# mLSTM denominators as four rows of one PSUM bank with one reciprocal in the next stage, and score products issued two steps ahead

## The chip, the cores and the metric

The kernel runs on one core of one Trainium2 chip. The metric is the device time of one execution in microseconds (us). The kernel before takes 2518.95 us, the median of three runs (2518.74 to 2519.68).

A core has a matrix engine (TensorE, "PE" in the profile, with its weight loads as "PEld"), a vector engine (VectorE, "DVE"), a scalar engine (ScalarE, "ACT"), GpSimd ("POOL") and SyncE ("SP"), which here only issues DMAs. Each runs its own instructions in order; semaphores tie them together. PE writes to PSUM, which has eight banks of 128 partitions by 512 floats; everything else lies in SBUF.

## What is computed

The reference is two blocks of a hybrid network, for a sequence of 512 tokens of width 1024. The first block has two layers, and each layer has three mixers: an mLSTM (four heads of width 256), a gated linear attention and a sparse attention. The change touches only the mLSTM and what stands around it. This is its step, which the reference runs chunk by chunk:

```python
bcum = jnp.cumsum(lfj, axis=-1)
dmat = jnp.where(causal, bcum[..., :, None] - bcum[..., None, :] + lij[..., None, :], -jnp.inf)
inter = bcum + m[..., None]
m_row = jnp.maximum(inter, jnp.max(dmat, axis=-1))
w_intra = jnp.exp(dmat - m_row[..., None])
w_inter = jnp.exp(inter - m_row)
s_qk = jnp.einsum('bhld,bhsd->bhls', qj, kj) * w_intra
num = jnp.einsum('bhls,bhse->bhle', s_qk, vj) + w_inter[..., None] * jnp.einsum('bhld,bhde->bhle', qj, C)
den = jnp.sum(s_qk, axis=-1) + w_inter * jnp.einsum('bhld,bhd->bhl', qj, n)
hj = num / jnp.maximum(jnp.abs(den), jnp.exp(-m_row))[..., None]
```

The output of a head is a weighted sum of values (`num`), divided per token by the larger of the absolute sum of weights (`den`) and `exp(-m_row)`. A normalisation over the head's 256 features and two gates follow.

## The kernel before, in words

The kernel computes the mLSTM for all 512 tokens at once, without chunks. Features lie on partitions and tokens along the free dimension. For a head `h` and a block `j` of 128 key tokens it makes a tile of weights `w` of 128 keys by the 512 - 128j queries at or after them. These sixteen pairs (h, j) are the *steps* of `mlstm_stage` (L909). The stage is run twice, once in each layer.

In a step:

- PE makes the scores, k transposed times q, in two matmuls over the head's two halves of 128 features (L939). `scores(n)` writes bank 1 or 2, in turn.
- DVE takes the row `G` of the head, which PE has spread over all partitions (L947, bank 0 or 7), subtracts a number per key and clamps (L999, `arguments`). ACT takes the exponential (L982).
- DVE multiplies scores and exponentials (L1025), masks the first 128 columns (L1028), and signals `w_ready`.
- PE multiplies `w` by the two halves of the values, into banks 3 and 4 (L963, L964: the numerators), and by a matrix of ones, into bank 5 (L967). So bank 5 holds the sum of weights of each token, the same in all 128 partitions.

PE issues `scores(n + 1)` just before it waits for `w` of step n. At j = 1 it also spreads the rows of the next head (`head_rows`): `G` (L947) and `em`, which is exp(-m_row) (L950, bank 6). L950 waits for `em_copied`, since bank 6 still holds the row of the current head until DVE has copied it to SBUF (L1032).

When the first step of the next head has its weights, DVE calls `finish` for the head before: it takes the larger of minus the sum and `em` (L1006), then the larger of the sum and that (L1009), then the reciprocal (L891), and multiplies the two tiles of the head's numerators by it (L895). Only behind that stands L1032. The numerators were copied out of banks 3 and 4 by ACT (L973) into `m.yT`; PE waits for this copy (`num_copied`) before it writes the next head's numerators. For the last head, the reciprocal and the two products are left to the next stage (`mlstm_last`, L898).

The next stage is a `product_stage`: PE multiplies the layer's input by weight granules in three split passes (L276), ACT and POOL split the weights in two parts (L293, L340), and *sides* put other work between. A side is a generator for each engine. PE calls all sides twice per granule (24 matmuls): at its start and at its half. DVE and ACT call theirs once per granule. Within one engine the order is fixed when the program is written: the rest of a side's turn stands behind whatever it waits for. On DVE the sides of this stage start with `mlstm_last`, then `topk_side` (L1366 and L1370, sixteen rounds that find the largest index scores of the sparse attention; L1376 ends it), then `dsa_norms` (L1277), which waits for ACT (L537). PE's L511 belongs to `dsa_norms`. PE uses banks 0 to 3 there; the sparse attention's side uses banks 4 to 6, from turn 12 on. Between two stages all engines meet at a barrier.

The matmuls of the mLSTM are in plain 32-bit floats. The trace shows each as two MATMUL records.

Of the kernel before, what the change touches and what calls it, by code (L numbers as in the profile page):

```python
# [8 lines left out]
ALU = mybir.AluOpType  # L9
# [3 lines left out]
P = 128  # L13
S = 512
# [874 lines left out]
def mlstm_over(m, dve, own, h):  # L889

    own.op(dve.reciprocal(m.rs[:, 2, :], m.rs[:, 1, :]))  # L891
    own.wait()
    for e in range(2):
        y = m.yT[:, 2 * h + e, :]
        own.op(dve.tensor_tensor(y, y, m.rs[:, 2, :], ALU.mult))  # L895


def mlstm_last(m):  # L898

    def vector(dve, sem):  # L900
        own = Chain(dve, sem["last_head"])
        mlstm_over(m, dve, own, ML_H - 1)
        own.wait()
        yield

    return Side(["last_head"], lambda pe, sem: iter(()), lambda act, sem: iter(()), vector)


def mlstm_stage(nc, m, ahead):  # L909
# [3 lines left out]
    em = ab  # L913

    with stage(nc, "rows_ready", "qk_ready", "arg_ready", "exp_ready", "w_ready", "num_done", "pv_done", "num_copied", "den_read",
               "raw_loaded", "high_ready", "low_ready",
               "em_copied", "dve_own") as (block, sem):
# [15 lines left out]
        def _(pe):  # L933
            def scores(n):
                h, j = steps[n]
                if n >= 2:
                    pe.wait_ge(sem["w_ready"], n - 1)
                for kk in range(2):
                    last = pe.matmul(m.ps[:, 1 + n % 2, 0:S - j * P], k[:, 2 * h + kk, j * P:(j + 1) * P],  # L939
                                     q[:, 2 * h + kk, j * P:S], start=(kk == 0), stop=(kk == 1))  # L940
                last.then_inc(sem["qk_ready"], 1)

            def head_rows(h):
# [44 lines left out]
        def _(dve):  # L988
# [13 lines left out]
            def finish(h):  # L1002

                dve.wait_ge(sem["em_copied"], h + 1)
# [1873 lines left out]
```

## Time and profile before

| | |
|---|---|
| median of three runs | 2518.95 us (2518.74 to 2519.68) |
| the profiled execution | 2534.25 us |
| its span, first to last instruction | 2532.5 us |
| PE busy in the span | 2369.5 us (94%) |
| DVE busy | 1214.2 us (48%) |
| ACT busy | 949.6 us (37%) |
| POOL busy | 817.3 us (32%) |
| mean clock granted to PE | 0.966 of full speed |
| first mLSTM stage, from PE's first matmul | 228.16 us |
| product stage behind it, from PE's first matmul | 301.88 us |
| second mLSTM stage, from PE's first matmul | 912.10 us |
| product stage behind it, from PE's first matmul | 984.43 us |

All times within the kernel are of the one profiled execution, counted from its first instruction. The profiled execution is 15.3 us (0.6%) longer than the median of the plain runs, and 1.75 us of it lie outside the span. A row of a timeline gives the start, the length, the engine, the line, the operation with what it writes and reads, and in brackets the engine's idle time before it and who ended it. Matmuls are pipelined, so their lengths overlap: the distance between two starts tells the pace.

### The profile page before, as it was taken

The numbers are of one execution on the slowest core, as the hardware profiler recorded it, in microseconds if no ns is written. First come the engines' busy times: TensorE is split into PE (matmuls) and PEld (weight loads), VectorE is DVE, ScalarE is ACT, GpSimd is POOL, SyncE is SP. The second block draws the span as 40 slices with busy tenths as digits, with TensorE's granted clock in tenths as the row PEclk, the third lists the DMA queues.
The fourth block names the chain that finished last, engine by engine and source line by source line (L and its number), as shares of the span: only waits on it lengthen the run. The fifth ranks groups of instructions, "written<-read, shape, count | busy, mean of one in ns | idle before, by whom it ended". The sixth has DMA issues, their size and how long they took to land. (4 is left out here: it accounts for less than half of the span.)

```text
span 2532.5 us, 39488 instructions
## 1 busy us (share of the span) xinstructions
PE 2369.5 (94%) x16764; PEld 1874.0 (74%) x16764; DVE 1214.2 (48%) x1966; ACT 949.6 (37%) x1385; POOL 817.3 (32%) x364
## 2 busy tenths in 40 slices
PE   5999899999999998999989989998999899999997
PEld 3877587786778866877768758887676678888886
DVE  2254764433332558543431457765454466605524
ACT  3432145544244322454342343332336624212233
POOL 1342033332433411333234322222332344444442
PEclk8999899999999999999999988999899999999998
DMA  3221022221222201222223210000221123323222
GB/s 126 76 92 50 25 83 75 67 76 58 93 77 75 92 34 43 83 76 67 67 67 105 92 34 3 4 3 9 88 72 62 59 89 102 100 93 99 98 94 75
DMA packets 50139, 176.31 MB, mean 70 GB/s; under 512 B 5604, under 2 KB 6188, under 8 KB 49964
## 3 DMA queue, kind: packets, MB, share of 16 engines
q1 hardware_dynamic: 49404, 172.78, 20.6%
q8 instruction: 133, 2.18, 0.4%
q10 hardware_dynamic: 560, 1.00, 0.1%
q14 instruction: 42, 0.34, 0.0%
HBM read 171.65 MB, written 2.11 MB: 69 GB/s over the span
## 5 line engine op out<-in xcount | busy, mean ns | idle before, releaser
L340 POOL TENSOR_TENSOR w_low<-work,w_high 128x1024 fp32r<-128x1024 f32 x310 | 752.9, 2429 | 1433.9 <-ACT w_high L293 1433.9
L276 PE MATMUL ps<-x_high_tiles,w_high 128*128 128x512 f32 x1640 | 665.8, 406 | 29.6 <-DVE x_low_tiles L657 10.5
L276 PE MATMUL ps<-x_low_tiles,w_high 128*128 128x512 f32 x1640 | 647.1, 395 | 0.8 <-DVE x_low_tiles L372 0.8
L276 PE MATMUL ps<-x_high_tiles,w_low 128*128 128x512 f32 x1640 | 647.7, 395 | 0.0
L293 ACT ACTIVATE w_high<-work 128x1024 fp32r<-128x1024 f32 x310 | 327.7, 1057 | 719.3 <-PE ps L276 717.7
L276 PEld LDWEIGHTS ps<-x_high_tiles,w_high 128*128 128x128 f32 x1640 | 312.6, 191 | 129.5 <-issue 54.5
L276 PEld LDWEIGHTS ps<-x_low_tiles,w_high 128*128 128x128 f32 x1640 | 312.7, 191 | 70.5 <-DVE x_low_tiles L383 1.7
L276 PEld LDWEIGHTS ps<-x_high_tiles,w_low 128*128 128x128 f32 x1640 | 312.6, 191 | 67.5 <-issue 5.3
L276 PE MATMUL ps<-arena_parts,w_high 128*128 128x512 f32 x1088 | 347.8, 395 | 13.6 <-POOL w_low L340 5.4
L276 PEld LDWEIGHTS ps<-arena_parts,w_high 128*128 128x128 f32 x1088 | 206.6, 190 | 60.9 <-issue 8.4
L276 PE MATMUL ps<-arena_parts,w_low 128*128 128x512 f32 x544 | 213.9, 393 | 0.0
L276 PE MATMUL ps<-w_high,x_high_tiles 128*128 128x256 f32 x576 | 169.0, 293 | 0.0
L276 PE MATMUL ps<-w_low,x_high_tiles 128*128 128x256 f32 x576 | 163.1, 283 | 0.0
L276 PE MATMUL ps<-w_high,x_low_tiles 128*128 128x256 f32 x576 | 163.0, 283 | 0.0
L444 DVE TENSOR_TENSOR xT_sb<-ps,xT_sb 128x512 f32<-128x512 f32 x40 | 27.6, 692 | 261.5 <-PE ps L276 261.5
L1674 PE MATMUL ps<-work 64*64 64x64 f32 x3584 | 118.8, 225 | 8.1 <-DVE work L1989 7.3
L1674 PEld LDWEIGHTS ps<-work 64*64 64x64 f32 x3584 | 113.9, 140 | 14.9 <-issue 14.8
L276 PEld LDWEIGHTS ps<-w_high,x_high_tiles 128*128 128x128 f32 x576 | 110.3, 192 | 14.0 <-issue 13.6
L276 PEld LDWEIGHTS ps<-arena_parts,w_low 128*128 128x128 f32 x544 | 103.4, 190 | 21.9 <-issue 0.7
L1892 POOL TENSOR_TENSOR work<-work,arena 128x512 f32<-128x512 f32 x40 | 54.6, 1380 | 193.9 <-ACT work L1866 101.2
L276 PEld LDWEIGHTS ps<-w_low,x_high_tiles 128*128 128x128 f32 x576 | 110.4, 192 | 2.5 <-issue 2.2
L276 PEld LDWEIGHTS ps<-w_high,x_low_tiles 128*128 128x128 f32 x576 | 110.4, 192 | 0.0
(428 smaller groups left out, 2855.5 us busy)
## 6 DMA issues: line engine op xcount, KB each, us to landing
work<-w_first SPq DMA_DIRECT2D x180, 512.0 KB, 3.7
work<-w_second SPq DMA_DIRECT2D x134, 512.0 KB, 3.7
xT_sb<-xT SPq DMA_DIRECT2D x8, 256.0 KB, 6.8
outT<-arena SPq DMA_DIRECT2D x8, 256.0 KB, 2.1
arena<-distance_bias SPq DMA_DIRECT2D x4, 256.0 KB, 3.6
small<-small SPq DMA_DIRECT2D x1, 819.5 KB, 4.3
arena<-consts SPq DMA_DIRECT2D x1, 544.0 KB, 3.7
base<-consts ACTq DMA_DIRECT2D x1, 512.0 KB, 5.9
```

Source lines behind the costliest of these rows:

```text
L276: ins = pe.matmul(out, lhsT, rhs, start=(n == 0 and k == 0 and q == 0), stop=(n == unit["granules"] - 1 and k == len(ops[i]) - 1 and q == 2))
L293: act.activation(m.wh[:, split_of(g), :], m.raw[:, raw_of(g), :], ACT.Copy).then_inc(sem["high_ready"], 1)
L340: pool.tensor_tensor(m.wl[:, split_of(g), :], m.raw[:, raw_of(g), :], m.wh[:, split_of(g), :].bitcast(F32), ALU.subtract).then_inc(sem["lo ...
L444: return dict(dve=lambda e, ps, own: e.tensor_tensor(dst, ps, dst, ALU.add))
L1674: ins = pe.matmul(out[HALF[p], cols], lhsT[HALF[p], cols], rhs[HALF[p], cols], start=True, stop=True)
L1892: pool.tensor_tensor(ch(w.L), ch(w.AT), every(w.lev[:, n * 64:n * 64 + 64]), ALU.mult).then_inc(sem[f"lev_ready{w.d}"], 1)
```

## The change

It does four things.

1. The denominators. The matmul with the matrix of ones is replaced by one with a block of four columns (`m.one_column[:, 3 - h:7 - h]`), in which column h is one and the others are zero. So head h adds its sums of weights to row h of bank 5 and zeros to the other rows; the bank collects all sixteen steps of the stage in four rows.
2. `em` is no longer spread over the partitions. L950 and L1032 and the waits around them go, and `finish` goes with its four operations a head. Bank 6 is free.
3. In the next product stage `mlstm_last` makes the larger values and one reciprocal for the four heads, on tiles of 4 by 512. PE spreads the four rows with four matmuls (banks 4 and 6, in turn), and DVE multiplies the eight tiles of numerators by them, from PSUM. DVE does heads 0 and 1 in its second turn and heads 2 and 3 in its third; PE spreads rows 0 and 1 at its fourth call and rows 2 and 3 at its sixth.
4. The scores get a third bank (1, 2 and 6), and PE issues `scores(n + 2)`, no longer `scores(n + 1)`, before it waits for `w` of step n.

Also the first square of `dsa_norms` on ACT no longer waits for `mlstm_last`.

```diff
-def mlstm_last(m):
+def mlstm_last(m, banks):
+    den, em, inv = m.ps[0:ML_H, 5, :], m.rows[0:ML_H, 1, :], m.rs[0:ML_H, 2, :]
 
     def vector(dve, sem):
-        own = Chain(dve, sem["last_head"])
-        mlstm_over(m, dve, own, ML_H - 1)
+        own = Chain(dve, sem["last_own"])
+        own.op(dve.scalar_tensor_tensor(out=inv, in0=den, scalar=-1.0, in1=em, op0=ALU.mult, op1=ALU.max))
         own.wait()
+        own.op(dve.tensor_tensor(inv, den, inv, ALU.max))
+        own.wait()
+        dve.reciprocal(inv, inv).then_inc(sem["den_inv"], 1)
+        for h in range(ML_H):
+            if h % 2 == 0:
+                yield
+            dve.wait_ge(sem["inv_spread"], h + 1)
+            for e in range(2):
+                y = m.yT[:, 2 * h + e, :]
+                dve.tensor_tensor(y, y, m.ps[:, banks[h % 2], :], ALU.mult).then_inc(sem["y_divided"], 1)
+        dve.wait_ge(sem["y_divided"], 2 * ML_H)
         yield
+
+    def tensor(pe, sem):
+        yield from turns(3)
+        pe.wait_ge(sem["den_inv"], 1)
+        for h in range(ML_H):
+            if h >= 2:
+                pe.wait_ge(sem["y_divided"], 2 * (h - 1))
+            pe.matmul(m.ps[:, banks[h % 2], :], m.pick[0:ML_H, h * P:(h + 1) * P], inv, start=True, stop=True).then_inc(sem["inv_spread"], 1)
+            if h == 1:
+                yield from turns(2)
...
@@ mlstm_stage, PE
             def scores(n):
                 h, j = steps[n]
-                if n >= 2:
-                    pe.wait_ge(sem["w_ready"], n - 1)
+                if n >= 3:
+                    pe.wait_ge(sem["w_ready"], n - 2)
...
-                pe.matmul(m.ps[:, (0, 7)[h % 2], :], m.pick[0:ML_H, h * P:(h + 1) * P], G, start=True, stop=True)
-                if h:
-                    pe.wait_ge(sem["em_copied"], h)
-                pe.matmul(m.ps[:, 6, :], m.pick[0:ML_H, h * P:(h + 1) * P], em, start=True, stop=True).then_inc(sem["rows_ready"], 1)
+                pe.matmul(m.ps[:, (0, 7)[h % 2], :], m.pick[0:ML_H, h * P:(h + 1) * P], G, start=True, stop=True).then_inc(sem["rows_ready"], 1)
 
             head_rows(0)
             scores(0)
+            scores(1)
             for n, (h, j) in enumerate(steps):
-                if n + 1 < len(steps):
-                    scores(n + 1)
+                if n + 2 < len(steps):
+                    scores(n + 2)
...
-                if h and j == 0:
-                    pe.wait_ge(sem["den_read"], h)
-                pe.matmul(m.ps[:, 5, j * P:S], m.ones, w, start=(j == 0), stop=(j == T - 1)).then_inc(sem["pv_done"], 1)
+                pe.matmul(m.ps[0:ML_H, 5, j * P:S], m.one_column[:, 3 - h:7 - h], w, start=(n == 0),
+                          stop=(n == len(steps) - 1)).then_inc(sem["pv_done"], 1)
@@ mlstm_stage, DVE
-            def finish(h):
...
-                if j == 0:
-                    if h:
-                        finish(h - 1)
-                    dve.tensor_copy(m.rs[:, 0, :], m.ps[:, 6, :]).then_inc(sem["em_copied"], 1)
-            finish(ML_H - 1)
@@ dsa_norms
-        if i == 0:
-            act.wait_ge(sem["last_head"], 3)
```

How the order moves. First PE at the start of an mLSTM stage. Before, L947 and L950 are the spread rows, L939 the scores, and L963, L964 and L967 the products with `w`:

```order
L947 MATMUL ps<-arena,base 128x512
L950 MATMUL ps<-arena,base 128x512
L939 MATMUL ps<-arena 128x512 x2
L939 MATMUL ps<-arena 128x384 x2
L963 MATMUL ps<-tmp,arena 128x512
L964 MATMUL ps<-tmp,arena 128x512
L967 MATMUL ps<-tmp,base 128x512
L939 MATMUL ps<-arena 128x256 x2
L947 MATMUL ps<-arena,base 128x512
L950 MATMUL ps<-arena,base 128x512
L963 MATMUL ps<-tmp,arena 128x384
```

The same place now (L965 is the spread of `G`, L957 the scores, L979 to L981 the products with `w`):

```order
L965 MATMUL ps<-arena,base 128x512
L957 MATMUL ps<-arena 128x512 x2
L957 MATMUL ps<-arena 128x384 x2
L957 MATMUL ps<-arena 128x256 x2
L979 MATMUL ps<-tmp,arena 128x512
L980 MATMUL ps<-tmp,arena 128x512
L981 MATMUL ps<-tmp,cols 4x512
L957 MATMUL ps<-arena 128x128 x2
L965 MATMUL ps<-arena,base 128x512
L979 MATMUL ps<-tmp,arena 128x384
```

Each pair of score matmuls has moved up by one step, and the second spread row is gone.

DVE where one head passes to the next, before (L999 arguments, L1025 and L1028 the weights, L1006 to L1032 the work on the head before):

```order
L999 TENSOR_SCALAR tmp<-ps,cols 128x384
L1025 SCALAR_TENSOR_TENSOR tmp<-ps,tmp 128x512
L1028 TENSOR_TENSOR tmp<-tmp,base 128x128
L1006 SCALAR_TENSOR_TENSOR rs<-ps,rs 128x512
L1009 TENSOR_TENSOR rs<-ps,rs 128x512
L891 RECIPROCAL rs<-rs 128x512
L895 TENSOR_TENSOR arena<-arena,rs 128x512 x2
L1032 COPY rs<-ps 128x512
L999 TENSOR_SCALAR tmp<-ps,cols 128x256
L1025 SCALAR_TENSOR_TENSOR tmp<-ps,tmp 128x384
```

and now (L1014 arguments, L1027 and L1030 the weights):

```order
L1014 TENSOR_SCALAR tmp<-ps,cols 128x384
L1027 SCALAR_TENSOR_TENSOR tmp<-ps,tmp 128x512
L1030 TENSOR_TENSOR tmp<-tmp,base 128x128
L1014 TENSOR_SCALAR tmp<-ps,cols 128x256
L1027 SCALAR_TENSOR_TENSOR tmp<-ps,tmp 128x384
```

Nothing stands between the weights of one head's first step and the arguments of the step after.

DVE at the start of the product stage behind, before (L891 and L895 for the last head, then the top-k rounds):

```order
L343 UNCONDITIONAL_BRANCH
L891 RECIPROCAL rs<-rs 128x512
L895 TENSOR_TENSOR arena<-arena,rs 128x512 x2
L1366 MAX arena<-arena 128x8 x3
L1370 MATCH_REPLACE arena<-arena 128x256
```

and now:

```order
L343 UNCONDITIONAL_BRANCH
L899 SCALAR_TENSOR_TENSOR rs<-ps,arena 4x512
L901 TENSOR_TENSOR rs<-ps,rs 4x512
L903 RECIPROCAL rs<-rs 4x512
L910 TENSOR_TENSOR arena<-arena,ps 128x512 x4
L1361 MAX arena<-arena 128x8 x3
L1365 MATCH_REPLACE arena<-arena 128x256
```

The first four products (L910) stand ahead of the first top-k round; four more stand behind the second round. On PE the first pair of spreads stands behind 36 of the stage's matmuls at L276, and the second pair behind 24 more.

## Rows read from the trace of the kernel before

**Rows 1.** The page, busy time of each engine.
```profile
PE 2369.5 (94%) x16764; PEld 1874.0 (74%) x16764; DVE 1214.2 (48%) x1966; ACT 949.6 (37%) x1385; POOL 817.3 (32%) x364
```
**Rows 2.** Windows over the two mLSTM stages: stretch, length, busy us (count), PE clock, DMA, GB/s.
```profile
228.00:302.00 74.00, 63.31 (x177) 34.67 (x178) 43.65 (x70) 14.34 (x23) 4.66 (x2) 0.84 0.06 22
912.00:985.00 73.00, 62.38 (x179) 34.97 (x180) 44.09 (x70) 14.34 (x23) 4.66 (x2) 0.86 0.06 22
```
**Rows 3.** Timeline of PE in the first stage, where it waits.
```profile
257.00 2.07 PE L950 MATMUL ps<-arena,base 4*128 4x512 f32 x2 [2.95 <-DVE rs L1032]
...
292.10 1.65 PE L963 MATMUL ps<-tmp,arena 128*128 128x384 f32 x2 [3.60 <-DVE tmp L1028]
```
**Rows 4.** Who waited for L1032 and for L1028, both stages: us, times.
```profile
  PE ps L950: 8.6, 4
...
  PE ps L963: 7.2, 2
```
**Rows 5.** Timeline of DVE, first stage, after the first step of the second head.
```profile
248.63 0.68 DVE L1006 SCALAR_TENSOR_TENSOR rs<-ps,rs 128x512 f32<-128x512 f32 x1
...
250.07 3.35 DVE L891 RECIPROCAL rs<-rs 128x512 f32<-128x512 f32 x1
253.46 2.88 DVE L895 TENSOR_TENSOR arena<-arena,rs 128x512 f32<-128x512 f32 x2
256.27 0.68 DVE L1032 COPY rs<-ps 128x512 f32<-128x512 f32 x1
```
**Rows 6.** Windows, PE alone: six stretches behind its waits, both stages, and their sum.
```profile
257.00:263.00 6.00, 6.00 (x8) 0.50 0.00 0
...
sum 28.70, PE 28.70; mean PE 4.78
```
**Rows 7.** Windows of PE over the first 8 us of each stage.
```profile
228.00:236.00 8.00, 7.84 (x11) 0.57 0.57 198
912.00:920.00 8.00, 7.90 (x15) 0.79 0.55 197
```
**Rows 8.** Timeline of the first stage around the copy of the first numerators.
```profile
248.08 1.02 ACT L973 ACTIVATE arena<-ps 128x1024 f32<-128x1024 f32 x1 [4.62 <-PE ps L964]
248.11 1.46 PE L939 MATMUL ps<-arena 128*128 128x384 f32 x4
...
249.40 0.59 PE L963 MATMUL ps<-tmp,arena 128*128 128x512 f32 x1
```
**Rows 9.** Timeline of PE, first stage: scores of 256 columns, then spread rows.
```profile
239.08 1.03 PE L939 MATMUL ps<-arena 128*128 128x256 f32 x4
240.03 1.12 PE L947 MATMUL ps<-arena,base 4*128 4x512 f32 x2
241.00 1.02 PE L950 MATMUL ps<-arena,base 4*128 4x512 f32 x2
```
**Rows 10.** Timeline where the first stage ends and the product stage begins.
```profile
299.13 1.02 ACT L973 ACTIVATE arena<-ps 128x1024 f32<-128x1024 f32 x1 [6.36 <-PE ps L964]
...
300.15 0.69 DVE L1009 TENSOR_TENSOR rs<-ps,rs 128x512 f32<-128x512 f32 x1
...
301.88 0.47 PE L276 MATMUL ps<-x_high_tiles,w_high 128*128 128x512 f32 x1 [2.56 <-PEq L90]
```
**Rows 11.** Timeline of PE in a product stage: a spread row ahead of L276.
```profile
492.74 1.12 PE L1056 MATMUL ps<-rs,base 4*128 4x512 f32 x2
493.79 0.50 PE L276 MATMUL ps<-x_high_tiles,w_high 128*128 128x512 f32 x1
```
**Rows 12.** Timeline of DVE in the first product stage: top-k begins, ends, and what follows.
```profile
306.59 1.48 DVE L1366 MAX8 arena<-arena 128x8 f32<-128x256 f32 x3
...
354.10 0.95 DVE L1376 TENSOR_SCALAR arena<-arena 128x256 f32<-128x256 f32 x3
373.73 2.74 DVE L1277 SCALAR_TENSOR_TENSOR arena<-arena,small 128x512 f32<-128x512 f32 x4 [18.68 <-ACT arena L537]
```
**Rows 13.** Timeline of PE where the first mLSTM stage begins.
```profile
228.16 1.09 PE L947 MATMUL ps<-arena,base 4*128 4x512 f32 x2 [1.35 <-PEq L90]
```

More of the change, by code:

```diff
@@ L886, in mlstm_gates @@
     return Side(["gates_dve", "gates_act", "z_ready", "log_ready", "u_ready", "u_turned"], tensor, scalar, vector)
[L889 to L895, printed above, removed]
-def mlstm_last(m):
+def mlstm_last(m, banks):
+    den, em, inv = m.ps[0:ML_H, 5, :], m.rows[0:ML_H, 1, :], m.rs[0:ML_H, 2, :]
     def vector(dve, sem):
-        own = Chain(dve, sem["last_head"])
-        mlstm_over(m, dve, own, ML_H - 1)
+        own = Chain(dve, sem["last_own"])
+        own.op(dve.scalar_tensor_tensor(out=inv, in0=den, scalar=-1.0, in1=em, op0=ALU.mult, op1=ALU.max))
         own.wait()
-        yield
-    return Side(["last_head"], lambda pe, sem: iter(()), lambda act, sem: iter(()), vector)
+        own.op(dve.tensor_tensor(inv, den, inv, ALU.max))
[9 more added lines that the diff above has]
+        dve.wait_ge(sem["y_divided"], 2 * ML_H)
+        yield
+    def tensor(pe, sem):
[7 more added lines that the diff above has]
+                yield from turns(2)
+    return Side(["last_own", "den_inv", "inv_spread", "y_divided"], tensor, lambda act, sem: iter(()), vector)
 def mlstm_stage(nc, m, ahead):
@@ L912, in mlstm_stage @@
     zf, ab, lf, F, u, G = mlstm_rows(m)
-    em = ab
-    with stage(nc, "rows_ready", "qk_ready", "arg_ready", "exp_ready", "w_ready", "num_done", "pv_done", "num_copied", "den_read",
+    sbank = (1, 2, 6)
+    with stage(nc, "rows_ready", "qk_ready", "arg_ready", "exp_ready", "w_ready", "num_done", "pv_done", "num_copied",
                "raw_loaded", "high_ready", "low_ready",
-               "em_copied", "dve_own") as (block, sem):
+               "dve_own") as (block, sem):
         steps = [(h, j) for h in range(ML_H) for j in range(T)]
@@ L935, in scores @@
                 h, j = steps[n]
-                if n >= 2:
-                    pe.wait_ge(sem["w_ready"], n - 1)
+                if n >= 3:
+                    pe.wait_ge(sem["w_ready"], n - 2)
                 for kk in range(2):
-                    last = pe.matmul(m.ps[:, 1 + n % 2, 0:S - j * P], k[:, 2 * h + kk, j * P:(j + 1) * P],
+                    last = pe.matmul(m.ps[:, sbank[n % 3], 0:S - j * P], k[:, 2 * h + kk, j * P:(j + 1) * P],
                                      q[:, 2 * h + kk, j * P:S], start=(kk == 0), stop=(kk == 1))
@@ L1024, in _ @@
                 w = m.tmp[:, 2 + n % 2, 0:S - j * P]
-                own.op(dve.scalar_tensor_tensor(out=w, in0=m.ps[:, 1 + n % 2, 0:S - j * P], scalar=256 ** -0.5, in1=a,
+                own.op(dve.scalar_tensor_tensor(out=w, in0=m.ps[:, sbank[n % 3], 0:S - j * P], scalar=256 ** -0.5, in1=a,
                                                 op0=ALU.mult, op1=ALU.mult))
@@ L2595, in second_and_next @@
             product_stage(nc, m, second_weights(layer) + weights_after, both + after, banks=4, begun=0, late=late, held=[last],
-                          side=together(mlstm_last(m), topk_side(m), dsa_norms(m, 7, start=2, q_jobs=0),
+                          side=together(mlstm_last(m, (4, 6)), topk_side(m), dsa_norms(m, 7, start=2, q_jobs=0),
                                         later(dsa_side(m, (4, 5, 6)), DSA_AT),
```

10 lines of the change are left out of this document (removed).

## The prediction

> **What bounds the kernel now.** I read the page first. PE is busy 94% of the span and every other engine at most half of it [rows 1], so a change counts only where it shortens PE's work or PE's idle time. Next I took windows over the two mLSTM stages, from their first matmul to the first of the product stage behind. There PE is busy 63.3 of 74.0 us and 62.4 of 73.0, and its granted clock is 0.84 and 0.86 on average, while DVE, at 43.7 and 44.1, is not full either [rows 2]. PE thus loses time there in two ways: it waits, and it runs at a lower clock. The reader is to see both in the next views.
>
> The timeline of PE shows the waits. Before L950 of the third head's rows PE stands for 2.95 us until L1032 has emptied bank 6, and late in the stage 3.60 us until L1028 has made a tile of weights [rows 3]. Over both stages the line views give 8.6 us in four waits for L1032 and 7.2 us in two for L1028 [rows 4]. The timeline of DVE shows why it is late: behind the first step of each head stand L1006, L1009, L891 and L895, from 248.63 to 256.3, and the copy L1032 is behind them all. The reciprocal alone is 3.35 us, the two products 2.88 here, where POOL works beside them [rows 5]. The next tile of weights stands behind this too, so L1028's 3.60 us have the same cause.
>
> The windows show what follows a wait. Six stretches behind the waits, 28.7 us in all, have PE fully busy at a granted clock of 0.50, which is the lower level of 1.2 GHz [rows 6]. Both stages also begin with such a stretch: clocks of 0.57 and 0.79 over their first 8 us are 6.9 and 3.4 us at the lower level [rows 7].
>
> **The change part by part.** *The waits.* L950 and L1032 no longer exist, and finish() is out of DVE's queue, so the 15.8 us of rows 4 go: **-15.8**. What is late next? I walked one handover between heads with the new order. PE now issues scores(n + 2) before it waits for w of step n. DVE may begin w(n) when the products of step n - 2 are done, and it is needed only after scores(n + 1), the products of step n - 1 and scores(n + 2). The shortest such cover is at n - 1 = (h, 3): 1.29 us of scores (248.11 to 249.40 [rows 8]), then three products over 128 columns (0.7), then scores of 256 columns (239.08 to 240.03, 0.95 [rows 9]), 2.9 us. DVE needs for it a multiplication over 512 columns, about as L1006 (0.68 [rows 5]), and a mask on 128, which is shorter: about 1.1 with the gaps. At the stage's end no scores are left, but then the tiles are narrow, and 1.3 us of products cover some 0.8 us. So DVE does not hold PE up in a step. ACT's copy of the numerators does come close: it starts when the last numerators are written (248.08) and ends at 249.10, and PE must wait for it. Before, PE had scores of 384 columns to do until 249.40 [rows 8]; now it has scores of 256, until 248.11 + 0.95 = 249.06. The wait is about 0.1 us, at six handovers: **+0.6**. Its ends are 0 and 0.4 (a copy seen 0.3 us late), 0 to 2.4 in all.
>
> *The clock.* In all six stretches of rows 6 PE does at half speed what takes half the time at 2.4 GHz, and each lies behind a wait that goes. With PE waiting for no more than tenths of a microsecond I expect none of them: 28.7 / 2 = **-14.4**. The ends are 0 (it falls all the same) and -19.5, if the stretches at the start of rows 7 went too (10.3 / 2 = 5.1 more). I take -14.4, since what comes before the stages' start is unchanged.
>
> *The spread rows.* Eight times L950 goes from PE's queue (four in each stage), at the distance of the twin row L947 to it, 240.03 to 241.00 = 0.97 [rows 9]: **-7.8**. In their place eight L920 of the same form come into the product stages, where PE is the bound and nothing hides them. A spread row ahead of L276 took 492.74 to 493.79 = 1.05 there [rows 11]: **+8.4**, with 0.97 as the other end (+7.8).
>
> *The sums over four columns.* L981 streams as many columns as L967 did; only its weights are narrower. The trace has 0.97 for a spread row and 0.95 for scores with the same number of columns but other weights [rows 9], so I take 0, with 0.1 us either way for each 512 columns, 20 of them: -2 to +2.
>
> *The end of a stage.* Before, DVE's L1009 ended it, at 300.84; ACT's copy ends at 300.15 [rows 10] and is now the last. The barrier comes 0.69 us sooner, twice: **-1.4**.
>
> *DVE in the product stage.* It starts with three operations on 4x512 tiles, which no row shows. The nearest have as many columns on 128 partitions, L1006 with 0.68 and L891 with 3.35 [rows 5]; I take them in full, 4.8 with L901, as the dear end, and a thirty-second of it would be the other. Then DVE waits for the spreads. PE comes to them after 36 matmuls of about 0.23 us (301.88 + 8.3 = 310.2), by which time the reciprocal is long done: PE does not wait. DVE has the first row at about 9.4 us after the stage's start, makes four products by 12.2, and only then begins top-k, which before began at 306.59 - 301.87 = 4.7 [rows 12]: 7.5 us late. Four more products behind the second round bring another 2.8 us, 10.3 in all. With L910 at its dearest, as the pair of L895 in rows 5 (1.44 each), it is 16. Behind top-k DVE is idle 18.68 us until ACT's L537 lets L1277 go [rows 12], so this slack takes all of it: **0**. Without that cover each microsecond would be paid on PE, since products of the sparse attention wait for L1277. Dropping ACT's wait for mlstm_last gives nothing: DVE was done with it long before ACT's turn.
>
> The sum: -15.8 - 14.4 - 7.8 + 8.4 + 0.6 - 1.4 = -30.4 us. Against the profiled execution's own 2534.25 (span 2532.5) that is 2503.9. The plain runs' median is 15.3 us lower; none of the terms should depend on that, so I forecast 2518.95 - 30.4 = **2488.5 us**.
>
> **The rivals.** *The clock falls at the handover into the product stage (B).* Between the last matmul and the barrier PE stands for 2.56 us before it starts at 301.88 [rows 10], and it came out at full clock. But at 228.16 it had waited only 1.35 us [rows 13] and then spent 6.9 us at the lower level [rows 7]. The two differ although the wait was shorter where the clock fell, so the moment matters and not the wait alone, and the change shifts the moment. If it falls, the first 6.4 us or so of the product stage run at half speed, 3.2 us lost, up to twice: 2491.7 to 2494.9. The Trainium skill, "TensorE: Matmul & The Clock Gate", section "What's actually happening", speaks for this rival: it says that the clock gate's observation period runs on by itself and is not restarted when a kernel begins its work, so the same work may come out with or without a slow stretch. By that rule the clock's term is not certain in either direction, and the stretches at the start of the stages are not either.
>
> *The start's slow stretches go as well (C).* Then the time is 2488.5 - 5.1 = 2483.4. For it speaks that they differ by a factor of two from one stage to the other [rows 7]; against it that nothing ahead of the first one changes.
>
> *A new wait takes the old one's place (D).* If PE stood a microsecond at each of the six handovers for the copy, with the clock falling as often as now, 6 us and the 14.4 would be lost again: 2508.9. For it speaks that the copy's margin is now negative by a hair [rows 8]; against it that such a wait would be tenths, and the clock fell only behind waits of over 1.3 us.
>
> *PE stays at the lower level through the mLSTM stages (E), the rival on the other side.* The stage starts at half clock, and this needs the clock not to come back. PE's matmuls in the first stage now take about 71 us (74.0 [rows 2] less the 2.6 ahead of 301.88 [rows 10]). Less 7.9 of waits, less half of the 13.9 us of rows 6 and the 6.9 of rows 7 that are its own, less 3.9 for the spread rows, 49 us are left at full rate. At half rate they are 98, 27 more than now, twice: 2519 + 54 + 8 for the new spreads = 2581. It makes the kernel slower from the point where the additional time at half rate passes 61 us in the two stages together (half of that is the gain of 30.4). Against it: in all cases of rows 6 and 7 the clock came back after 3 to 7 us of full work.
>
> **How the numbers follow.** Chances: forecast 0.62, B 0.18, C 0.06, D 0.10, E 0.04. About 5 us (0.2%) is what a measurement of this kernel can tell from no change. All of the first four are faster by far more: faster 0.95, within 0.2% 0.01 (D gone further), slower 0.04. The unknown terms around the forecast, 2 us for the narrow sums, 0.6 for the spreads and up to 1.8 for the copy, with small shifts of the clock elsewhere, give 2484 to 2493. To hold the time 8 times in 10 the range takes in B and most of C, and leaves D and E out: 2480 to 2498.
>
> **What would show it.** In the profile after: no wait of PE over half a microsecond within the mLSTM stages, and their windows at a clock of 1.00 from 8 us on (the clock's term); 52 to 55 us from the first matmul of a stage to the first of the next, where there were 73.7 and 72.3; L981 at the distance of L967; the copy wait at L979 of each head's first step near 0.1 us (if it is a microsecond, D). In the product stages eight L920 about a microsecond each; DVE idle some 4.5 us ahead of L910, top-k ending about 10 us later than before counted from the stage's start, and L1277's new line still let go by ACT. If DVE is busy up to it, the slack was not enough and the zero for DVE was wrong. If the stages shrink by 20 us each and the kernel's time by much less, something behind them gave it back, and the forecast is wrong there.

## The result, and the profile after

The changed kernel takes 2500.13 us (median of 4 runs, 2496.68 to 2500.59), the kernel before in the same rounds 2519.31 (2518.74 to 2525.36): a ratio of 0.9921, 95% interval 0.9907 to 0.9936. That is 19 us less by the medians and 20 by the ratio. The forecast was 30.4 us less, 2488.5, with a range of 2480 to 2498. The direction held; the size didn't.

The profiled execution after took 2499.92 us (span 2498.1, clock 0.976), as long as the median. The one of before was 15 us over its median. The busy times, which answer to [rows 1]:

```profile
PE 2354.1 (94%) x16764; PEld 1850.6 (74%) x16764; DVE 1182.3 (47%) x1940; ACT 948.7 (38%) x1385; POOL 817.3 (33%) x364
```

The windows over the first mLSTM stage, the second, and the product stages behind each, in that order (from PE's first matmul to the next stage's; the first two answer to [rows 2]):

```profile
228.00:284.00 56.00, 54.49 (x168) 24.27 (x168) 21.16 (x48) 13.87 (x23) 4.71 (x2) 0.97 0.08 29
895.30:951.40 56.10, 54.56 (x169) 24.49 (x169) 21.29 (x49) 13.86 (x23) 4.72 (x2) 0.97 0.08 28
284.00:895.30 611.30, 589.55 (x2962) 474.12 (x2963) 269.25 (x482) 250.98 (x377) 211.29 (x88) 0.99 0.22 76
951.40:1473.60 522.20, 496.88 (x2371) 393.09 (x2371) 241.06 (x438) 214.53 (x312) 178.22 (x74) 0.98 0.22 77
```

PE's busy time fills the mLSTM stages but for 1.5 us, and DVE's has halved. The whole list of PE's waits in the first of them (us, times, longest), where [rows 3, 4] had waits for L1032 and L1028, is the wait for the stage's own beginning:

```profile
PE ps L965 <- PEq L90: 1.4, 1, 1.4
```

The lower clock is left over the first 8 us only, as in [rows 7]. Two windows of PE alone, in the first stage:

```profile
228.00:236.00 8.00, 7.98 (x18) 0.79 0.57 198
236.00:284.00 48.00, 46.51 (x152) 1.00 0.00 1
```

The handover between two heads, in PE's timeline (it answers to [rows 8, 9]). L957 makes the scores, L979 and L980 the numerators, L981 the sums over four columns:

```profile
246.04 0.39 PE L979 MATMUL ps<-tmp,arena 128*128 128x128 f32 x2
246.26 0.39 PE L980 MATMUL ps<-tmp,arena 128*128 128x128 f32 x2
246.58 0.38 PE L981 MATMUL ps<-tmp,cols 128*4 128x128 f32 x2
246.89 1.13 PE L957 MATMUL ps<-arena 128*128 128x256 f32 x4
247.86 1.09 PE L979 MATMUL ps<-tmp,arena 128*128 128x512 f32 x2
248.79 1.02 PE L980 MATMUL ps<-tmp,arena 128*128 128x512 f32 x2
249.74 1.02 PE L981 MATMUL ps<-tmp,cols 128*4 128x512 f32 x2
250.69 0.71 PE L957 MATMUL ps<-arena 128*128 128x128 f32 x4
```

L979 of the next head starts 0.97 us after the scores, so it doesn't wait for ACT's copy. But from start to start, L980 to L981 takes 0.95 us and L981 to L957 0.95 as well. Before the change, the next matmuls with whole weights followed at 0.86 (285.76 L964, 286.62 L967, 287.47 L939, quoted below). Over 128 columns the distances are 0.32 and 0.31 where L979 to L980 is 0.22. So it costs PE about 0.1 us each way to go to the four-column weights and back, at both widths.

DVE where the product stage begins and where its slack was (it answers to [rows 12]; L899 to L903 are `mlstm_last`, L910 its products, L1361 top-k, L1274 the line that was L1277):

```profile
284.03 0.68 DVE L899 SCALAR_TENSOR_TENSOR rs<-ps,arena 4x512 f32<-4x512 f32 x1 [3.31 <-PEq L90]
284.74 0.68 DVE L901 TENSOR_TENSOR rs<-ps,rs 4x512 f32<-4x512 f32 x1
285.46 3.34 DVE L903 RECIPROCAL rs<-rs 4x512 f32<-4x512 f32 x1
293.56 2.48 DVE L910 TENSOR_TENSOR arena<-arena,ps 128x512 f32<-128x512 f32 x4 [4.76 <-PE ps L920]
295.96 1.47 DVE L1361 MAX8 arena<-arena 128x8 f32<-128x256 f32 x3
...
360.16 2.74 DVE L1274 SCALAR_TENSOR_TENSOR arena<-arena,small 128x512 f32<-128x512 f32 x4 [12.57 <-ACT arena L537]
```

L1274 is still let go by ACT, 76.1 us after the stage's start; before it was 71.9 (373.73 - 301.88 in [rows 10, 12]). ACT itself is later by the spread rows and DVE has 12.57 us left. The spread rows, in PE's timeline ahead of L276 (as [rows 11]):

```profile
292.40 1.98 PE L920 MATMUL ps<-rs,base 4*128 4x512 f32 x4
294.31 0.50 PE L276 MATMUL ps<-x_high_tiles,w_high 128*128 128x512 f32 x1
```

Two rows take 1.91 us, so 0.96 each, the lower end of the forecast.

### The profile page after: what moved, and what is told of

It reads as the page before. It is cut to its first block and busy times, and to the rows that moved or that the text cites. A ratio compares the mean times of both kernels' runs of the same rounds, so it can differ in the third digit from the quotient of the medians.

```text
span 2498.1 us, 39444 instructions
## 1 busy us (share of the span) xinstructions
PE 2354.1 (94%) x16764; PEld 1850.6 (74%) x16764; DVE 1182.3 (47%) x1940; ACT 948.7 (38%) x1385; POOL 817.3 (33%) x364
## 5 line engine op out<-in xcount | busy, mean ns | idle before, releaser
L276 PE MATMUL ps<-x_high_tiles,w_high 128*128 128x512 f32 x1640 | 665.1, 406 | 28.6 <-DVE x_low_tiles L657 10.5
L276 PE MATMUL ps<-x_low_tiles,w_high 128*128 128x512 f32 x1640 | 645.6, 394 | 0.8 <-DVE x_low_tiles L372 0.8
L276 PE MATMUL ps<-x_high_tiles,w_low 128*128 128x512 f32 x1640 | 645.2, 393 | 0.0
L276 PEld LDWEIGHTS ps<-x_high_tiles,w_high 128*128 128x128 f32 x1640 | 312.1, 190 | 131.7 <-issue 56.4
L276 PEld LDWEIGHTS ps<-x_low_tiles,w_high 128*128 128x128 f32 x1640 | 311.2, 190 | 70.2 <-DVE x_low_tiles L383 1.7
L276 PEld LDWEIGHTS ps<-x_high_tiles,w_low 128*128 128x128 f32 x1640 | 312.1, 190 | 67.4 <-issue 5.3
L276 PE MATMUL ps<-arena_parts,w_high 128*128 128x512 f32 x1088 | 345.4, 392 | 13.5 <-POOL w_low L340 5.4
L276 PEld LDWEIGHTS ps<-arena_parts,w_high 128*128 128x128 f32 x1088 | 205.0, 188 | 60.3 <-issue 8.4
L276 PE MATMUL ps<-arena_parts,w_low 128*128 128x512 f32 x544 | 212.2, 390 | 0.0
L276 PE MATMUL ps<-w_high,x_high_tiles 128*128 128x256 f32 x576 | 168.8, 293 | 0.0
L276 PE MATMUL ps<-w_low,x_high_tiles 128*128 128x256 f32 x576 | 162.9, 283 | 0.0
L276 PE MATMUL ps<-w_high,x_low_tiles 128*128 128x256 f32 x576 | 162.8, 283 | 0.0
L276 PEld LDWEIGHTS ps<-w_high,x_high_tiles 128*128 128x128 f32 x576 | 110.2, 191 | 14.0 <-issue 13.6
L276 PEld LDWEIGHTS ps<-arena_parts,w_low 128*128 128x128 f32 x544 | 102.6, 189 | 21.7 <-issue 0.7
L276 PEld LDWEIGHTS ps<-w_low,x_high_tiles 128*128 128x128 f32 x576 | 110.4, 192 | 2.5 <-issue 2.2
L276 PEld LDWEIGHTS ps<-w_high,x_low_tiles 128*128 128x128 f32 x576 | 110.3, 192 | 0.0
```

The lines of the kernel that those rows point to most:

```text
L276: ins = pe.matmul(out, lhsT, rhs, start=(n == 0 and k == 0 and q == 0), stop=(n == unit["granules"] - 1 and k == len(ops[i]) - 1 and q == 2))
```

## The experiments

The theory after the result had three parts: the four-column sums cost PE time; the cost of DVE's part in the product stage was nothing, as forecast; and the clock's term was read from an execution with more slow clock than most. The rivals were a cost of the division's new place, or of the third score bank, and chance between executions. Ratios are to the kernel before in the same rounds (2520.24 us for the first four runs, 2521.53 for the next four).

**The two kernels again.** Both unchanged.

> The unchanged kernel once more, for a second trace of it. Theory A (the number of slow-clock stretches differs between executions of one program, and the execution that was profiled for the prediction had more than usual): times near 2519 us, mean granted clock about 0.972 where the first trace has 0.966, and the difference in time between the two traces (about 15 us) made up of time at half clock, half of each stretch, with the waits of 15.8 us unchanged. Rival B (the profile itself made that execution longer): clock again about 0.966 in any trace, time 2534 us when profiled. Ratio to before 1.000.

> The changed kernel once more. 2500 us if the first measurement stands (ratio 0.992); clock 0.976. Each mLSTM stage 56 us from its first matmul to the next stage's first. If the clock's stretches vary from execution to execution, this trace differs from the first by multiples of some 1.7 us, outside the waits.

Measured: the kernel before 2519.51 us (2515.09 to 2527.57, 12 runs), ratio 0.9991 (0.9975 to 1.0008). The change 2501.49 (2494.4 to 2506.45), ratio 0.9917 (0.9892 to 0.9941). So the result stands. One program's executions differ by more than 10 us: those of the kernel before in the same rounds went from 2514.23 us (clock 0.975) to 2534.51 (clock 0.966). The clock is rounded, but taking time times (1 - clock) off each leaves 2450.6 us on average for 17 runs of before and 2442.0 for 6 of the change. Hence 8.6 of the 19 us are not the clock's, and 10.5 are: the medians of what is taken off are 70.5 and 60.0. The 12 other runs of the kernel before give 2451.2 and 68.0, so each share is known to some 2 us.

The trace of the kernel before in these runs is of the longest of the 12, 2527.57 us at a clock of 0.969. Its mLSTM stages took 73.6 us (227.95 to 301.54) and 72.3 (911.70 to 984.05), with the same waits and the same slow stretches as the forecast's execution: the window from 290 to 298 us, behind L1028's wait, has a clock of 0.57 in both. By itself it could not tell whether these stretches are in every execution. The profiled execution of the change had mLSTM stages of 54.4 us each, at full clock from end to end:

```profile
227.80:282.20 54.40, 52.87 (x169) 23.75 (x169) 21.20 (x49) 13.87 (x23) 4.72 (x2) 1.00 0.09 30
893.40:947.80 54.40, 52.85 (x169) 23.75 (x169) 21.18 (x49) 13.89 (x23) 4.71 (x2) 1.00 0.08 29
```

**Whole weights for the sums.** A pattern of zeros with ones in column 127 gives 128-column weights in place of the four-column ones. The sums still land in rows 0 to 3 of bank 5, and its other rows get zeros.

```diff
+            pool.memset(m.rs[:, 0, 0:2 * P], 0.0).then_inc(sem["pattern"], 1)
+            pool.wait_ge(sem["pattern"], 1)
+            pool.memset(m.rs[:, 0, P - 1:P], 1.0).then_inc(sem["pattern"], 1)
...
-                pe.matmul(m.ps[0:ML_H, 5, j * P:S], m.one_column[:, 3 - h:7 - h], w, start=(n == 0),
+                if n == 0:
+                    pe.wait_ge(sem["pattern"], 2)
+                pe.matmul(m.ps[:, 5, j * P:S], m.rs[:, 0, P - 1 - h:2 * P - 1 - h], w, start=(n == 0),
```

> The change, but the sums use a weight tile of 128 columns (one column of ones, 127 of zeros) in place of 4 columns. Theory C (a matmul whose weights have 4 columns costs about 0.1 us when PE changes to it and 0.1 us when it changes back, 32 steps): 6 us less than the change, 2494 us (ratio to before 0.990), and 0.86 us per 512 columns from L980 to L981 and on to the scores. Rival (the extra 0.1 us comes from something else, such as the PSUM bank): no difference.

Measured: 2491.65 us (2487.1 to 2498.08), ratio 0.988 (0.9856 to 0.9905): 9.8 us less than the change. Its second stage, at full clock (the window), and the sums in the first (the timeline, L986):

```profile
893.40:943.50 50.10, 48.16 (x167) 28.19 (x166) 21.26 (x48) 13.13 (x23) 4.72 (x2) 1.00 0.09 32
```

```profile
240.37 0.81 PE L983 MATMUL ps<-tmp,arena 128*128 128x384 f32 x2
241.01 0.81 PE L986 MATMUL ps<-tmp,rs 128*128 128x384 f32 x2
241.66 1.88 PE L960 MATMUL ps<-arena 128*128 128x512 f32 x4
243.37 0.59 PE L982 MATMUL ps<-tmp,arena 128*128 128x256 f32 x2
...
246.63 1.03 PE L960 MATMUL ps<-arena 128*128 128x256 f32 x4
247.77 1.10 PE L982 MATMUL ps<-tmp,arena 128*128 128x512 f32 x2
```

The same place in the changed kernel, for which L980 starts at 239.87:

```profile
240.61 0.81 PE L981 MATMUL ps<-tmp,cols 128*4 128x384 f32 x2
241.34 1.98 PE L957 MATMUL ps<-arena 128*128 128x512 f32 x4
243.17 0.59 PE L979 MATMUL ps<-tmp,arena 128*128 128x256 f32 x2
```

L986 follows L983 at 0.64 us and L960 follows at 0.65. In the changed kernel the same two distances are 0.74 and 0.73. The scores behind the sums are longer there too: 1.83 us from L957 to L979, against 1.71 from L960 to L982. From L968 at 892.7 us, where the second stage starts, to the next stage at 943.5 are 50.9 us against 54.4. So the narrow sums cost 3.5 us a stage, 7 in all. The medians of the two kernels differ by more, 9.8, and those of the folded pair below, which differ by the same edit, by 6.0.

The rows account for the 3.5. A step with narrow sums is some 0.29 us longer: 0.10 on the way in, 0.09 on the way out and 0.1 in the scores behind. Fifteen such steps and the way into the last are 4.45. Against that the whole weights lose something at each of the three handovers between heads. There L982 starts 1.14 us after its scores (246.63 to 247.77), which need 0.86 (four times the 0.215 of a record over 256 columns, from L983 at 243.81 to L986 at 244.24), and 0.15 us behind the end of ACT's copy of the numerators (246.60 to 247.62). So PE waits some 0.28 for the copy, 0.8 in a stage, and 3.6 are left.

**One score tile ahead.** PE makes the scores one step ahead, as before the change. The edit leaves `sbank[n % 3]` as it is, so the scores still go round three banks.

```diff
-                if n >= 3:
-                    pe.wait_ge(sem["w_ready"], n - 2)
+                if n >= 2:
+                    pe.wait_ge(sem["w_ready"], n - 1)
...
-            scores(1)
...
-                if n + 2 < len(steps):
-                    scores(n + 2)
+                if n + 1 < len(steps):
+                    scores(n + 1)
```

> The change with scores(n + 1) again before the wait, two banks in turn. Theory (the gain in the mLSTM stages comes from DVE's queue, and the lookahead only covers tenths): PE waits about 1 us where a head passes to the next and little elsewhere, each stage 1 to 4 us longer than with the change, time 2503 to 2508 us. Rival F (the lookahead is what took the waits away): the two stages are each 6 us or more longer, 2514 us or above.

Measured: 2499.55 us (2492.56 to 2508.56), ratio 0.9909 (0.9884 to 0.9934), no difference from the change. The windows of the two stages:

```profile
227.70:282.00 54.30, 52.77 (x169) 23.39 (x169) 22.24 (x49) 13.82 (x23) 4.80 (x2) 1.00 0.09 30
894.60:950.50 55.90, 54.34 (x169) 24.27 (x169) 22.35 (x49) 13.89 (x23) 4.80 (x2) 0.97 0.08 29
```

The first is as short as the change's at full clock, and PE has no wait in it behind its start: the waits of about 1 us that were expected at the handovers aren't there. The second step of lookahead gave nothing, once the long work had left DVE. Since three banks are still in use, this run says nothing on the rival of the third bank. Against that one speak the scores with whole weights, which use three banks and take 1.71 us for two matmuls over 512 columns, the pace of 0.86 from before the change.

**The change without the division.** `mlstm_last` is left out of the product stage, and so the division by the denominators.

```diff
-                          side=together(mlstm_last(m, (4, 6)), topk_side(m), dsa_norms(m, 7, start=2, q_jobs=0),
+                          side=together(topk_side(m), dsa_norms(m, 7, start=2, q_jobs=0),
```

> The change without mlstm_last: the denominators are summed but the numerators are not divided (that part of the computation is left out). Theory D (the eight spreads are paid on PE at about 1.05 us each and DVE's lateness is free): 8.4 us less than the change, 2492 us. Rival E (the product stage gave back the missing gain, since top-k is late by 10 us or the spreads disturb the weights' flow): 15 to 20 us less, 2480 to 2485 us.

Measured: 2489.79 us (2488.59 to 2493.09), ratio 0.9876 (0.9852 to 0.9901): 11.7 less than the change. Eight spread rows at 0.96 are 7.7 of it. What the rest is takes executions with nearly equal losses to the clock in these stages, which come further down. The windows of the two product stages here:

```profile
281.70:891.00 609.30, 587.51 (x2955) 474.73 (x2955) 259.07 (x471) 251.16 (x377) 211.49 (x88) 0.98 0.23 76
947.00:1465.80 518.80, 493.47 (x2362) 392.67 (x2363) 230.12 (x427) 214.65 (x312) 178.45 (x74) 0.98 0.24 77
```

**Before without reciprocal and products.** In the kernel before, DVE skips L891 and L895 for all heads (the division is left out), and nothing else changes.

```diff
 def mlstm_over(m, dve, own, h):
-    own.op(dve.reciprocal(m.rs[:, 2, :], m.rs[:, 1, :]))
...
+    return
...
-            act.wait_ge(sem["last_head"], 3)
+            pass
```

> The kernel before without the reciprocals and the products with them (the division is left out), all else as before: L1006, L1009 and L1032 and both spread rows stay. Theory G (the long part of DVE's queue was the waits' cause): the waits for L1032 and L1028 fall from 15.8 us to under 2, and the slow stretches behind them go; about 16 us of waits and about 10 us of clock less, 2494 to 2498 us. Rival H (the spread row and its copy alone hold PE up): waits of 5 us or more remain, over 2505 us.

Measured: 2496.07 us (2493.95 to 2497.06), ratio 0.9894 (0.9872 to 0.9916). The stages:

```profile
228.00:284.00 56.00, 53.45 (x177) 30.23 (x177) 30.78 (x60) 14.15 (x23) 4.71 (x2) 0.97 0.08 29
895.70:950.10 54.40, 51.84 (x177) 29.69 (x177) 30.77 (x60) 14.21 (x23) 4.71 (x2) 1.00 0.08 29
```

They are as short as with the whole change, with L950, L1032 and one tile of lookahead still there, and no wait for L1032 or L1028 is left in them. So what held PE up was the reciprocal with its two products ahead of L1032 in DVE's queue, and that alone. That the lengths are equal is a balance of two other things: four more spread rows make these stages some 3.4 us longer, and sums with whole weights make them 3.5 shorter.

**The division folded into the norm.** The norm behind it divides by the root of the mean square of a head's outputs. With d the denominator, dividing the undivided numerators by the root of (their sum of squares + 256 EPS d²) / 256 gives the same normalized values, so the reciprocal, the spread rows and a stage's eight products are not needed. One operation on 4x512 and one addition take their place. The second kernel has the whole weights for the sums as well.

```diff
-        dve.reciprocal(inv, inv).then_inc(sem["den_inv"], 1)
...
+        own.op(dve.scalar_tensor_tensor(out=floor, in0=floor, scalar=256 * EPS, in1=floor, op0=ALU.mult, op1=ALU.mult))
...
-        act.wait_ge(sem["ml_sum"], ML_H)
-        act.activation(rstd, m.ps[0:ML_H, bank, :], ACT.Ln, bias=m.eps[0:ML_H, :], scale=1.0 / 256).then_inc(sem["ml_log"], 1)
+        act.wait_ge(sem["ml_floor"], 1)
+        act.activation(rstd, rstd, ACT.Ln, scale=1.0 / 256).then_inc(sem["ml_log"], 1)
...
+        dve.wait_ge(sem["ml_sum"], ML_H)
+        dve.tensor_tensor(rstd, rstd, m.ps[0:ML_H, bank, :], ALU.add).then_inc(sem["ml_floor"], 1)
```

> The change, but the numerators are never divided: the denominator d enters the normalisation behind, as 1/sqrt(mean square + eps d^2), which is the same number. No reciprocal, none of the eight spreads L920, none of the sixteen products L910; one product and one sum on 4x512 tiles more in each layer. By the theory that the spreads are paid on PE in full (8.4 us, and what the division's absence showed, up to 11): 2490 us, ratio to before 0.988. Rival (the sum of squares must now wait for a step on DVE, which is behind the sparse attention's work there): 2 to 5 us of that are lost in a wait of ACT's L1052 and PE's spread of the norm.

> The same, and the sums with weight tiles of 128 columns. If the two savings add (6 to 7 us for the weights, 8.4 for the spreads): 2484 us, ratio to before 0.986; mLSTM stages of 51 us, or 53 with a slow stretch at their start.

Measured: folded 2489.79 us (2489.11 to 2490.48), ratio 0.987 (0.9848 to 0.9892); with whole weights 2483.79 (2481.99 to 2484.2), ratio 0.9845 (0.9823 to 0.9867). The first is as fast as the change without any division, so the folded form costs nothing that can be measured. The second is faster than both kernels, 16 to 18 us below the change and 38 below the kernel before. DVE at the start of the product stage of the first of them (L1342 is top-k):

```profile
281.73 0.68 DVE L894 SCALAR_TENSOR_TENSOR rs<-ps,arena 4x512 f32<-4x512 f32 x1 [3.31 <-PEq L90]
282.45 0.68 DVE L896 TENSOR_TENSOR rs<-ps,rs 4x512 f32<-4x512 f32 x1
283.16 0.68 DVE L898 SCALAR_TENSOR_TENSOR rs<-rs 4x512 f32<-4x512 f32 x1
283.87 1.48 DVE L1342 MAX8 arena<-arena 128x8 f32<-128x256 f32 x3
```

**More executions of the same two kernels.** What was open by then is whether the slow stretches that the forecast counted are in every execution. Neither kernel is changed.

> The kernel before, unchanged, once more with a trace, to see where its executions of 2514 to 2520 us have less of the lower clock than the one of 2534. If the four slow stretches that the forecast counted are in every execution, the mLSTM stages are again 73.6 and 72.4 us with 22 us lost to the lower clock, and an execution below 2525 differs in other stages. If they vary (the rival), these stages are shorter than 72 us in an execution below 2520.

> The same as before_look_1, another execution. In every one, the span less the time lost to the lower clock (the sum of each slow stretch times one less its clock) should be 2445 to 2448 us: then the executions differ by the clock alone.

> The same as before_look_1, a third execution, with the same numbers expected: 73.6 and 72.4 us if the slow stretches are fixed, less than 72 if they vary.

> The changed kernel once more with a trace. Its mLSTM stages are 54.4 us without a slow stretch or 56.1 with the one at the start, and the span less the time lost to the lower clock is 2438 to 2441 us, 7 less than before, where the forecast had 16 less. Rival: the stages of a slower execution have slow stretches at the handovers too.

Measured, one execution each: 2516.66, 2522.61 and 2518.35 us for the kernel before, 2498.44 for the change. The three mLSTM pairs of before took 70.8 and 69.2, 69.2 and 69.2, and 69.3 and 69.2 us, where the execution that the forecast was read from had 73.7 and 72.3. So the stretches vary, and the rival held. These executions were traced as well and lie near the median, so it isn't the tracing that makes one long. The waits don't vary: 8.6 us for L1032 and 7.2 for L1028 in every one. PE late in the first stage, in the profiled execution of the forecast:

```profile
285.76 1.02 PE L964 MATMUL ps<-tmp,arena 128*128 128x512 f32 x2
286.62 1.02 PE L967 MATMUL ps<-tmp,base 128*128 128x512 f32 x2
287.47 1.03 PE L939 MATMUL ps<-arena 128*128 128x256 f32 x4
...
293.53 1.49 PE L964 MATMUL ps<-tmp,arena 128*128 128x384 f32 x2
```

and in the third of the new executions, where the first row shows the same wait as [rows 3], and a window of PE around it:

```profile
289.98 0.91 PE L963 MATMUL ps<-tmp,arena 128*128 128x384 f32 x2 [3.60 <-DVE tmp L1028]
290.73 0.81 PE L964 MATMUL ps<-tmp,arena 128*128 128x384 f32 x2
...
292.02 0.61 PE L939 MATMUL ps<-arena 128*128 128x128 f32 x4
```

```profile
290.00:298.00 8.00, 5.45 (x26) 1.00 0.00 0
```

The wait is 3.60 us in both. In one PE comes out of it at half clock, L964 over 384 columns being 1.49 long, in the other at full, 0.81. The same happened in the second stage. So two of the six stretches, those behind the waits for L1028, were not in the second and third of the new executions; in the first a part of one was. Of the five traces of the kernel before, the two of long executions (2534 and 2528 us) have them whole, and the three near the median don't. A little later PE does slow down: in the third execution the window from 298 to 302 us, where the product stage has begun, has a clock of 0.57. The product stages as a whole lose as much in either, 10.2 us in the first of them. In the profiled execution of the forecast each lasted some 5.3 us from the wait's end (292.10 [rows 3]) until the clock was back (a window of PE from 292.10 to 297.40 has 0.50), which cost 2.65 us each. The rest of what these stages are shorter by is mostly the start of the first one, 3.4 us at half clock where it had 6.9 [rows 7].

These executions also price the division. The product stages of the third and of the change's had nearly the same loss to the clock (10.2 and 10.2 us before, 10.2 and 11.2 after, each the sum of the slow stretches times one less their clock). Before, then the change:

```profile
297.10:907.20 610.10, 588.30 (x2955) 475.16 (x2955) 265.30 (x474) 251.09 (x377) 211.49 (x88) 0.98 0.23 76
976.40:1495.80 519.40, 494.10 (x2363) 393.00 (x2363) 236.34 (x430) 214.61 (x312) 178.42 (x74) 0.98 0.24 77
```

```profile
283.50:898.00 614.50, 592.90 (x2963) 476.41 (x2963) 269.23 (x482) 251.07 (x377) 211.45 (x88) 0.98 0.23 75
952.30:1476.10 523.80, 498.61 (x2370) 394.46 (x2371) 239.97 (x438) 214.60 (x312) 178.32 (x74) 0.98 0.23 76
```

They grow by 4.4 us each, and PE's busy time by 4.6 and 4.5, with four more spread rows in each. PE's idle time doesn't grow (21.8 us, then 21.6, in the first). DVE's being late therefore costs nothing. Of the 8.8 us the eight rows are 7.7, and the second stage's slower clock 0.9. The matmuls beside a pair of spread rows grow too: the last L276 ahead of L920 takes 0.32 us (292.08 to 292.40, in the trace of the result) and the first behind it 0.34 (294.31 to 294.65), where 0.23 is usual. For four pairs that is another 0.8, and the three together are within a microsecond of the 8.8. Against the kernel without the division these two stages are 5.2 and 5.0 us longer, all of it in PE's busy time: 10.2 of the 11.7 measured. With 7.7, 0.9 and 0.8 as above, 0.8 of the 10.2 are left that no row tells, and so are the 1.5 outside these stages. The expectation on the span less the clock's loss was 2438 to 2441 for the change; it came out at 2442.8, and for the kernel before at 2445 to 2451 rather than 2445 to 2448. The loss that falls into a wait costs nothing, so this sum is good to some 3 us, no better.

## Why the prediction was wrong

The mechanism was right, and two terms of the sum were mis-sized. The larger error is the term of the sums over four columns, 0 with 2 us either way. It is +7: 54.4 us of a stage at full clock against 50.9 with whole weights. The rows it was taken from, a spread row against scores, have weights of 128 columns both (4 by 128 and 128 by 128, [rows 9]) and never go from one number of columns to another. They bound nothing of what was asked, and the range of 2 us had no row behind it. The trace had a sign all the same. Between whole weights 512 columns took 0.86 us (L964 to L967, 285.76 to 286.62), and both rows of the comparison, 0.95 and 0.97, stand next to a spread row, whose weights have four partitions. A change in the weights' shape had a price of some 0.1 us on either side, and comparing two rows that both paid it hid it.

The second is the clock's term, -14.4, with the sentence that carried it over to the median: that none of the terms should depend on which execution is read. This one does. Two of the six stretches, worth 5.3 us, were in the profiled execution and not in those near the median; that leaves 9.1. The trace alone could not tell which, but it was a warning that the profiled execution was 15.3 us over the median of the same program. Profile against profile, the change gained 34.3 us (2534.25 to 2499.92), more than the 30.4 of the forecast; at the medians it gained 19 to 20. The other 7 to 8 us by which the profiled execution was long lay in stages that the change doesn't touch: the stage behind the second product stage had 266.5 us and has 261.4 in the third of the new executions, and what follows it 762.2 and 759.4.

By step. The stages were forecast at 53.6 us each, or 51.0 less their slow starts. Measured at full clock is 54.4, and 50.9 with whole weights: the rest of the arithmetic for these stages came out right as a whole.

- *The waits*, -15.8: right. None is left, and the cause named, the reciprocal and products in DVE's queue, is shown by the kernel that leaves them out.
- *The spread rows removed*, -7.8: a little less. L965 alone takes 1.05 (238.07 to 239.12 in the changed kernel), where the pair of L947 and L950 took 1.91 before (240.03 in [rows 9] to 241.94, the start of L963). So eight times 0.86 went, 6.9.
- *The spread rows added*, +8.4: 7.7 by their rows, 8.8 with what goes beside them. Right within a microsecond.
- *The copy*, +0.6: nothing, its lower end, and that by luck. What the narrow sums cost covers the copy. With whole weights PE waits 0.28 us for it at each handover, 1.7 in six, which is within the 0 to 2.4 of the forecast but three times its 0.6. *The stage's end*, -1.4: the idle time there went from 2.56 us [rows 10] to 1.52 (before PE's first matmul at 284.03), so -2.1.
- *DVE in the product stage*, 0: right, with the forecast's 4.5 us of idle time (4.76), top-k later by 7.2 us (11.9 against 4.7 after the start) and L1274 still waiting for ACT. The reciprocal took its dear end, 3.34.

The sum at the median: -15.8 - 9.1 - 6.9 + 7 + 7.7 - 2.1 = -19.2, and measured are 19 and 20. Several terms are known to a microsecond at best (with 8.8 for the division the sum is -18.1), so that it comes this close is in part chance.

Of the rivals, C happened in part. Of three traces of the change one has the slow stretch at the start of both stages, one at one, and one at none. B didn't: the product stages of the change lose no more to the clock than those of before. D didn't, as the copy makes no wait, nor did E. The rule under B, the Trainium skill, "TensorE: Matmul & The Clock Gate", section "What's actually happening", that the clock gate's period runs on by itself, so that the same work may come out with or without a slow stretch, agrees with these traces: one wait of 3.60 us, once with 5.3 us of half clock behind it and once without. The prediction priced it under a rival only; it belonged to the term itself, whose likely value then lies below all that this one long execution showed.

## What to carry to other kernels

Before a gain is read from slow-clock stretches in one execution, compare that execution's time and clock with the median. Where it is far above, some of its stretches are not in the typical one, and a gain from them counts only in part. When a long operation stands in a queue ahead of a short one that PE waits for, move the long one first, and then ask whether the rest of the change is still needed; here neither the second step of lookahead nor the narrow sums paid. A new term wants a row that does the new thing: two rows that share a cost don't show it. A division in front of a scale-invariant norm can be folded into its epsilon; here that was as fast as leaving the division out.

## What the runs showed of the hardware

- A matmul with four-column weights between matmuls with whole ones costs about 0.1 us on the way in and 0.1 on the way out, at 128, 384 and 512 columns alike (0.95 against 0.86 at 512, 0.74 against 0.64 at 384, 0.32 against 0.22 at 128), and another 0.1 in the matmuls behind (1.83 against 1.71). It was 7 us in 32 of them by the stages' lengths.
- Weights of four partitions cost the matmuls beside them about 0.1 us as well: L276 takes 0.32 us ahead of a pair of spread rows and 0.34 behind it, and 0.23 elsewhere.
- A reciprocal takes 3.34 us on 4 partitions by 512 and 3.35 on 128 by 512 ([rows 5]). At 512 columns it made no difference that only 4 partitions of 128 were used.
- One program's executions spread over 20 us (2514.23 to 2534.51, 0.8%) with the clock's mean from 0.975 to 0.966. Waits were the same to 0.01 us where they were compared.
